# A two-block transformer kernel: x loaded and turned alone, weights split ahead of norms, and the second block's modulation summed between other products

## The reference

```
for i in range(DEPTH):
    mod_lat = (silu(c) @ w_mod[i] + b_mod[i])      # 6144 values: sh1, sc1, gt1, sh2, sc2, gt2
    mod_ctx = (silu(c_ctx) @ w_mod[i] + b_mod[i])
    hc = modulate(rms_norm_2(x_ctx, g_norm1[i]), csh1, csc1)   # modulate: h * (1 + scale) + shift
    h  = modulate(rms_norm_2(x_lat, g_norm1[i]), sh1, sc1)
    ... input projection, attention over both streams, pooling, mix ...
    x_lat = x_lat + gt1 * mix
    x_lat = x_lat + gt2 * sq_relu_mlp(modulate(rms_norm_2(x_lat, g_norm2[i]), sh2, sc2), w_mlp1[i], w_mlp2[i])
    if not last: the same for x_ctx
```

## Time and profile before

| | |
|---|---|
| median of 3 runs | 2930.61 us |
| the runs | 2924.84 to 2932.65 us |
| the profiled execution, its own time | 2934.35 us |
| its span, first to last instruction | 2932.6 us |
| mean granted clock | 0.954 |
| TensorE, VectorE, ScalarE, POOL busy | 94%, 52%, 30%, 3% of the span |
| data moved | 415.47 MB, 142 GB/s on the mean |

### The profile page before, as it was taken

How to read it: one execution, slowest core, us unless ns; L and a number is a source line. 1 busy time by engine, 2 the same in 40 slices (tenths; PEclk the granted TensorE clock), 3 DMA queues, 4 the chain that set the end, 5 groups by cost and what they waited for, 6 DMA issues and landing times. The chain is left out here.

```text
span 2932.6 us, 42259 instructions
## 1 busy us (share of the span) xinstructions
PE 2746.5 (94%) x17731; PEld 2370.5 (81%) x17731; DVE 1517.5 (52%) x2131; ACT 878.1 (30%) x1141; POOL 99.1 (3%) x179
## 2 busy tenths in 40 slices
PE   6999988999989999889999979899899999879998
PEld 6998887889989998778889934355799997636898
DVE  5774553427867844543257721452555553244555
ACT  3332201123333322101223321442333332243332
POOL 1100000000100000000001000000000000000000
PEclk8999989999999999989999989889999999989999
DMA  6775201635766764005347552000355455210452
GB/s 224 264 257 173 87 1 44 201 112 181 268 213 231 264 206 138 1 1 187 114 155 254 201 203 86 29 1 29 101 175 194 148 184 198 78 43 15 144 173 86
DMA packets 279067, 415.47 MB, mean 142 GB/s; under 512 B 10057, under 2 KB 235545, under 8 KB 277266
## 3 DMA queue, kind: packets, MB, share of 16 engines
q1 hardware_dynamic: 259948, 348.17, 36.1%
q0 software_dynamic: 18128, 64.20, 6.4%
q10 hardware_dynamic: 854, 1.13, 0.1%
HBM read 399.82 MB, written 13.65 MB: 141 GB/s over the span
## 5 line engine op out<-in xcount | busy, mean ns | idle before, releaser
L533 PE MATMUL ps<-h_high,w_high 128*128 128x256 f32 x1408 | 403.2, 286 | 17.1 <-DVE h_low L1169 10.3
L534 PE MATMUL ps<-h_low,w_high 128*128 128x256 f32 x1408 | 402.6, 286 | 0.0
L535 PE MATMUL ps<-h_high,w_low 128*128 128x256 f32 x1408 | 402.4, 286 | 0.0
L1190 DVE TENSOR_TENSOR w_low<-ring,w_high 128x2048 fp32r<-128x2048 f32 x132 | 302.1, 2290 | 136.1 <-ACT w_high L986 135.7
L629 PE MATMUL ps<-h_sb,ring 128*128 128x256 f32 x1472 | 328.0, 384 | 15.9 <-issue 9.3
L2404 DVE TENSOR_TENSOR w_low<-ring,w_high 128x2048 fp32r<-128x2048 f32 x96 | 219.8, 2291 | 222.9 <-ACT w_high L2231 222.9
L986 ACT ACTIVATE w_high<-ring 128x2048 fp32r<-128x2048 f32 x132 | 251.7, 1914 | 267.0 <-DMA ring<-in_ffn_w_in 152.6
L629 PEld LDWEIGHTS ps<-h_sb,ring 128*128 128x128 f32 x1472 | 282.9, 193 | 59.1 <-issue 17.3
L533 PEld LDWEIGHTS ps<-h_high,w_high 128*128 128x128 f32 x1408 | 274.8, 195 | 18.6 <-issue 11.4
L2231 ACT ACTIVATE w_high<-ring 128x2048 fp32r<-128x2048 f32 x96 | 183.9, 1915 | 313.6 <-PE ps L1935 313.6
L534 PEld LDWEIGHTS ps<-h_low,w_high 128*128 128x128 f32 x1408 | 274.8, 195 | 0.0
(11 more groups left out here) (380 smaller groups left out, 4654.8 us busy)
## 6 DMA issues: line engine op xcount, KB each, us to landing
ring<-in_w_mlp SPq DMA_DIRECT2D x96, 1024.0 KB, 5.3
ring<-in_ffn_w_in SPq DMA_DIRECT2D x88, 1024.0 KB, 8.5
wmod<-in_w_mod POOLq DMA_DIRECT2D x96, 512.0 KB, 6.5
ring<-in_ffn_w_out SPq DMA_DIRECT2D x44, 1024.0 KB, 5.0
ring<-in_w_mix_in SPq DMA_DIRECT2D x26, 1024.0 KB, 5.6
ring<-in_xattn_w_kv SPq DMA_DIRECT2D x16, 1024.0 KB, 5.4
mod_scratch<-mod_acc POOLq DMA_DIRECT2D x24, 512.0 KB, 5.5
ring<-mod_scratch SPq DMA_DIRECT2D x12, 1024.0 KB, 7.8
```

Source lines behind the costliest of these rows:

```text
L533: mm(dst, w_hi, x_hi, start=start, stop=False, **more)
L534: mm(dst, w_hi, x_lo, start=False, stop=False, **more)
L535: return mm(dst, w_lo, x_hi, start=False, stop=stop, **more)
L1190: v.tensor_tensor(w_low[:, slot, :], ring[:, slot, :], w_high[buffer], ALU.subtract).then_inc(w_low_ready.sem, 1)
```

## The change

In the front there is no block and no barrier any more. x is turned first, the squares follow on ScalarE (into `kt`, since `h_sb` holds the tokens), and the parameter rows are turned behind the sums of squares. Both tiles of the first feed-forward step are split ahead of the root (`first_high`, `first_low`); `cond` is made behind mem's norm. SP issues six weight tiles in place of three, POOL its loads, at once.

At the end of the first block SP loads the modulation's six tiles for layer 0 into the first block's ring (`MOD_SLOTS`, by when the slots come free). The second block sums two of them before the last norm's sums, one behind it, two behind the transposes, and the last behind the sums of both streams' first norm. Layer 1's tiles go through the second ring: two are summed ahead of the context's MLP of layer 0, four between the two MLPs (`MOD_BESIDE`), with the context's norm of layer 1 behind them. `mods` and `scls` are kept per layer.

In the output stage the sums of squares stand between the output tiles, the first two weight tiles are split ahead of the residual, and `scale` and `low` alternate per k. The MLP's first up tile goes k by k over both halves, its last down tile bank by bank (`acc_done`), and a start flag takes the place of the cleared banks. The output leaves in four quarters, of which ScalarE copies one.

```diff
 MEM_BANKS = (5, 6, 7, 0)
+MOD_SLOTS = (3, 4, 5, 0, 1, 2)
...
+MOD_BESIDE = ((0, 1), (2, 3, 4, 5))
...
     def _(pe):
+        pe.wait_ge(const_loaded.sem, 16)
+        pe.wait_ge(loaded.sem, 16)
+        for q in range(4):
+            for k in (2 * q, 2 * q + 1):
+                for h in range(2):
+                    at = (k % 2) * T + h * P
+                    last = nc.tensor.transpose(ps[q][:, at:at + P], x_tok[:, h, k * P:(k + 1) * P], ident)
+            last.then_inc(*x_turned.up())
         tensor_program(pe)
...
             if n == 0 and l == 0:
-                w_high_part(FfnTiles(0, 0), 0, 0, 0, 0)
+                act.wait_ge(*rows_turned.at(0, 1))
+                first_high(0, 0)
             act.wait_ge(*ss_done.at(l, n + 1))
...
+        sp.wait_ge(mod_stored.sem, MOD_CHUNKS * 16)
+        for s in MOD_SLOTS:
+            sp.wait_ge(w_used[s].sem, DEPTH * FIRST_USES[s] + 1)
+            c, t = divmod(s, MOD_THIRDS)
+            sp.dma_start(ring[:, s, :], scratch["mod"][0, :, c, t * SLOT:(t + 1) * SLOT]
+                         ).then_inc(store["v_loaded"][s].sem, 16)
...
+        def mod_sums(i, n, first, final):
+            r, used = loaded(("mod", i, n))
+            if i == 0:
+                r = store["ring"][:, n, :]
+            for m in range(SLOT // PIECE):
+                row = n * (SLOT // PIECE) + m
+                last = mm(ps[7][0:MOD_ROWS, :], one_row[:, MOD_ROWS - 1 - row:2 * MOD_ROWS - 1 - row],
+                          r[:, m * PIECE:(m + 1) * PIECE], start=(first and m == 0),
+                          stop=(final and m == SLOT // PIECE - 1))
+            last.then_inc(used.sem, 1)
...
-            norm(i, 1, streams(i))
-            for c in streams(i):
-                mlp(i, c)
-            layer_ends(i)
+                if j:
+                    for s in streams(i):
+                        sums(i, 1, s, j - 1)
+            for s in streams(i):
+                sums(i, 1, s, 3)
+            if i < DEPTH - 1:
+                for n in MOD_BESIDE[CTX]:
+                    mod_sums(i + 1, n, n == 0, False)
+            mlp(i, streams(i)[0])
+            if i < DEPTH - 1:
+                for n in MOD_BESIDE[LAT]:
+                    mod_sums(i + 1, n, False, n == MOD_BESIDE[LAT][-1])
+                for q in range(4):
+                    sums(i + 1, 0, CTX, q)
+                mod_turn(i + 1)
+                mlp(i, LAT)
+                for q in range(1, 4):
+                    sums(i + 1, 0, LAT, q)
...
+            mlp(i, streams(i)[0])
+            if i < DEPTH - 1:
+                w_low_part(MlpTiles(i, LAT), 0, 0, 0, 0)
+                residual(CTX)
+                w_low_part(MlpTiles(i, LAT), 0, 1, 1, 1)
                 dve.wait_ge(*x_ready.now(0))
-            layer_ends(i)
+                modulate(i + 1)
+                for k in range(KD):
+                    scale(i + 1, 0, CTX, k)
+                mlp(i, LAT)
+            residual(LAT)
```

More of the change, by code:

```diff
@@ L288, in build_first @@
     ring = sb("ring", [P, RING, SLOT])
+    store["ring"] = ring
     h_sb = sb("h_sb", [P, KD, T])
@@ L957, in norm @@
         def norm(l, n):
-            squares = cat if n == 3 else h_sb
+            squares = squares_of(l, n)
             if n == 3 or (n == 0 and l):
@@ L1580, in build_first @@
+    half = [name for name, _ in PARAMS[:9]]
     block = ctx.enter_context(nc.Block())
@@ L1583, in _ @@
     def _(sp):
+        sp.dma_start(x_tok, w_dram["x"].rearrange("o (h p) n -> p (o h) n", p=P)).then_inc(loaded.sem, 16)
+        sp.dma_start(cst["all"], w_dram["consts"]).then_inc(const_loaded.sem, 16)
+        load_rows(sp, [name for name, _ in PARAMS if name not in half])
         sync_program(sp)
@@ L1768, in build_second @@
     turned, placed = sig("second_turned"), sig("second_placed")
-    w_loaded = [sig(f"v_loaded{s}") for s in range(RING2)]
+    w_loaded = store["v_loaded"]
     w_used = [sig(f"v_used{s}") for s in range(RING2)]
@@ new lines, in square, with root @@
+        def square(i, n, s):
+            for q in range(4):
+                act.wait_ge(*x_ready.at(*x_needed(i, n, s, q)))
+                go(squares[s][:, 2 * q:2 * q + 2, :], xs[s][:, 2 * q:2 * q + 2, :], ACT.Square
+                   ).then_inc(*sq_ready.up())
+        def root(i, n, s):
+            act.wait_ge(*ss_done.at(i, norm_at(i, n, s) + 1))
+            go(std[:, s, :], norm_sum(i, n, s), ACT.Ln, bias=eps[:, 0:1], scale=1.0 / D).then_inc(*std_ready.up())
+            act.wait_ge(*std_ready.now(0))
+            go(std[:, s, :], std[:, s, :], ACT.Exp, scale=-0.5).then_inc(*std_ready.up())
@@ new lines, in shift, with first_high @@
+        def shift(i, n, s, k):
+            act.wait_ge(*scaled.at(i, scaled_at(i, n, s, k)))
+            dst = h_high[s][:, k, :] if n else h[:, k, cols(s)]
+            go(dst, h[:, k, cols(s)], ACT.Identity, bias=mods[i][:, s, n * 3 * KD + k:n * 3 * KD + k + 1]
+               ).then_inc(*h_ready.up())
+        def first_high(tiles):
+            if tiles.index:
+                s, use = place(("mlp2", tiles.i, CTX, MLP_STEPS - 2))
+                w_high_part(tiles, 0, 0, 0, 0, (w_used[s].sem, use + 1))
+                s, use = place(("mlp2", tiles.i, CTX, MLP_STEPS - 1))
+                w_high_part(tiles, 0, 1, 0, 1, (w_used[s].sem, use + 1))
+            else:
+                w_high_part(tiles, 0, 0, 0, 0)
+                w_high_part(tiles, 0, 1, 0, 1)
@@ L2240, in tile @@
                     before = tiles.used(*before)
-                elif tiles.index:
-                    s, use = place(("mlp2", i, streams(i)[tiles.index - 1], MLP_STEPS - 1))
-                    before = (w_used[s].sem, use + 1)
                 w_high_part(tiles, r, q, j, parity, before)
@@ L2273, in scalar_program @@
             ub, ask = unit_base(i), asked(i)
-            norm(i, 0, (CTX, LAT))
+            if i == 0:
+                for s in (CTX, LAT):
+                    square(i, 0, s)
+                for s in (CTX, LAT):
+                    root(i, 0, s)
+                for k in range(KD):
+                    for s in (CTX, LAT):
+                        shift(i, 0, s, k)
+            else:
+                square(i, 0, LAT)
+                root(i, 0, LAT)
+                for k in range(KD):
+                    shift(i, 0, LAT, k)
             for n, (j, _, width) in enumerate(IN_TILES):
@@ L2410, in tile @@
             def tile(r, q, j, t, parity, before):
-                if not (tiles.index == 0 and isinstance(t, int) and t == 1):
+                if not (isinstance(t, int) and t == 1):
                     w_low_part(tiles, r, q, t, parity)
```

460 lines of the change are left out of this document (234 added, 226 removed).

## The result

After takes 2843.95 us (median of 4, 2842.53 to 2863.51) against 2931.58 before (2924.84 to 2932.65): ratio 0.9724, interval 0.9695 to 0.9754. I had forecast 2871 and a range of 2862 to 2884.

The account below looks back on a forecast made before the run. TensorE, busy 94% of the span, was taken as the bound; 4.6 + 15.9 + 33.3 + 2.1 + 3.7 = 59.6 us off 2934.35 gave 2874.8, or 2871 us beside the median 2930.6. Range: 2862 to 2884.

Parts of the forecast that it names:

- Front: Start up to the first feed-forward matmul: earlier transposes and sums bring it from 34.1 to 29.5 us, saving 4.6 us.
- My upper bound, 6: Largest saving given for the start of the kernel: 6 us, if the clock rises within the sums.
- Between the blocks: First block's last matmul to first input projection: modulation matmuls cover waits, lost time falls from 20.8 to 4.9, saving 15.9 us.
- Layer 0 to layer 1: Block two, layer 0's MLPs to layer 1's projection: 36.2 us lost, new idle 2.9, saving 33.3 us.
- Layer 1's MLP 2.1 and the end 3.7: Shorter `h_low` wait at the last MLP saves 2.1 us; output by banks and quarters, with ScalarE's copy, saves 3.7 us.
- Its whole worth is TensorE time that was idle or slow at seven seams: Basis of the sum: no weight matmul removed or added; only seam time counts, less new waits, 59.6 us in all.
- signs that I had named for the profile after: First `h_high` matmul at 28 to 31 us, shorter seams, no idle between layer 0's MLPs, block two's waits under 5 us.
- rival C: The shorter pauses left (1.7 to 2.9 us) leave the clock up, saving more behind the projections: 2865 us; chance 0.12.
- Rival A: The sum of seam savings holds as it stands, 2871 us within some 5 us; chance 0.60.
- B's holes: Covers taken for full have holes, such as a late split tile; two of 3 us cost 10 us: 2881; chance 0.22.
- D's late tiles: Modulation tiles wait in SP's queue behind MLP weights and cover nothing: 2925 us, no change; chance 0.03.
- E's tiring clock: A fuller TensorE is granted less clock, in the MLPs from 2080 us on: slower, up to 2946 us; chance 0.03.

Follow-up runs that it names:

- e11: After, with two extra ScalarE squares of x ahead of its first squares, so that TensorE pauses between transposes and sums: 2859.41 us.
- e7: After, with ScalarE's three loads in layer 1 of the first block again issued ahead of the squares of the first norm: 2857.27 us.
- e3: Before, with filler matmuls of constants in the two pauses ahead of block two's score and value matmuls, four per layer: 2911.64 us, ratio 0.9938.
- e12: After, with filler matmuls of constants that fit the attention-stage pauses of block two, and more at three of its seams: 2826.93 us, ratio to before 0.9650.
- e10: After, with extra ScalarE squares to put a pause back ahead of both input projections of block two (missed its place in layer 0): 2860.05 us.
- e15: After, with three half-width filler matmuls (1.28 us) behind the first input projection tile of layer 0: 2868.30 us.
- e6: After, with two filler matmuls of 0.86 us each behind the first input projection tile, in both layers: 2856.98 us.
- e17: After, with the tile by tile wait undone: TensorE waits for all of h ahead of the first input tile, both layers: 2876.55 us.
- e16: Before, with only the tile by tile wait for the latents' shifted h in the first input tile added: 2921.35 us, ratio 0.9969.
- e1: The kernel before, unchanged, traced a second time: 2931.18 us.
- e5: Before, with two filler matmuls of 0.86 us each behind the first input projection tile, in both layers: 2932.84 us.
- e13: Before, with one half-width filler matmul (0.43 us) behind the first input projection tile of layer 0 alone: 2931.55 us.
- e14: Before, with two half-width filler matmuls (0.86 us) behind the first input projection tile of layer 0: 2929.74 us.
- e4: After, with too many filler matmuls in all five larger pauses of each attention stage of block two, running over the pauses: 2848.24 us.

## Why the prediction was wrong

The sum had the right sign and the right seams, and it was short by 30 us in the profiled executions (27 in the medians): 26 of the 30 in stages for which it had no term.

- **Front, 4.6 forecast, 8.5 measured.** The step that failed is "the sums, whose squares ride behind the copies, 6.4 at the low clock". That 6.4 was the price behind a pause of 4.84 us; after has none there, and they took 3.62. e11 put the pause back and got 5.94. My upper bound, 6, named this case but priced it at half. The other 1.2 us: they began at 12.2, not 12.8, and the chain behind them was 0.6 shorter.
- **Between the blocks, 15.9; measured 15.3.** Right, pause by pause (1.66, 0.87, 2.45 for 1.7, 0.9, 2.3).
- **Layer 0 to layer 1, 33.3; measured 33.7.** Right. The MLPs and the modulation run without a gap, no split tile and no residual came late:

```profile
2039.47:2241.00 201.53, 201.53 (x1584) 1.00 0.56 193
2241.00:2425.00 184.00, 184.00 (x1533) 1.00 0.52 174
```

- **Layer 1's MLP 2.1 and the end 3.7; measured 2.2 and 4.0.** Right.
- **The sum as a whole, and the larger failure.** The step is "Its whole worth is TensorE time that was idle or slow at seven seams": it took for granted that what the change does not touch keeps its length and its clock. It did not: the value stages gave 14.9 and 6.3 us, the projection and norms of layer 0 took 1.9 back (mean granted clock 0.90, before 0.91), and layer 1 of the first block gave some 3 to 4 through an edit that I left out (ScalarE's three loads behind the squares; of that the pause, 1.6 us, is shown in e7, the rest is read off two of its executions). The first block scatters by itself: 1647.6 to 1654.0 us in eight traces of before and its variants (mean 1651.3), 1645.2 to 1650.6 in ten of after's (mean 1647.0, e7 left out), so of the 5.7 in the two traces about 4 belong to the change.

Of the signs that I had named for the profile after, all came but one: the first `h_high` matmul stood at 25.6, not at 28 to 31.

What stands behind the 21 us, and how firmly. Shown: the low stretch is entered at the two pauses ahead of the stage (e3, and e12 beside e10), and the same code falls into it or not with 0.6 us of difference in where the clock stands on arrival (e7, one trace, beside four of after's seam). Delays of 1.3 and 1.7 us at the first input tile bring it back too (e15, e6). Shown too: in this change the tile by tile start of the projection is needed for value stages at 2.4 GHz (e17) and does not bring them about alone (e16). So the 21 us came by the moment of arrival, at which no step of the change aimed: as a design they are luck, and four fillers per layer gave before the same two lengths (e3). Argued only: how before corrects a delay. Several of its low stretches begin inside a pause of fixed length; if a start comes later, the pause ends later and less work falls into the stretch, so about half of the delay is given back, at each such stretch. That fits 0.38 of 0.43, 0.80 of 0.98 and all of 1.7 us. It would make the arrival of each kernel a fixed point, and before's lies on the side of the fall. This fits it too: in six traces with before's code up to there (before, e1, e3, e5, e13, e14) the low stretch about the first projection begins 2.8 to 3.1 us ahead of it, in eight with after's (all but e7) 1.4 to 1.6, although the first block's length differs by 6 and by 5 us among them. Open: which other edits move after's point to the other side, and why e6 fell with its last rise at 4.04 us, 0.02 from a trace that did not.

The Trainium skill, TensorE: Matmul & The Clock Gate (Why this matters for your kernels), asks that pauses be kept short. Here the clock stayed up through a pause of 1.66 us, and it fell at pauses of 2.45 and 2.23 us, which are shorter than those that the page warns of; the measurement decides. Windows from the end of the first of these pauses to the fall, and behind it:

```profile
1675.69:1711.70 36.01, 34.31 (x118) 1.00 0.65 230
1711.90:1718.50 6.60, 5.17 (x6) 0.50 0.94 298
```

So rival C, too, was wrong in its premise, although its time, 2865, lay nearer. Rival A's mechanism was right at the seams and missed the rest; B's holes, D's late tiles and E's tiring clock did not show.

## What to carry to other kernels

Cut the trace into stages and look at each for its granted clock, also at those that a change leaves alone: a stage of small matmuls behind a pause may run at either clock for tens of microseconds, and a shift of under 2 us elsewhere can switch it. Where that is so, guard the entry with fillers that fit the pause. It gave 18 us to before; in after, whose value stages were fast already, fillers in the pauses of norms and seams gave 17. Fillers longer than the pauses took their gain back (e4). And don't carry a duration over to a place with another pause ahead of it.

## What the hardware showed that I had not expected

- TensorE stayed at 1.2 GHz for 33.75 us while 33.62 of them were busy, on matmuls of 64 to 128 rows and 128 to 256 columns, and ran the same work at 2.4 GHz when it came in fast. The Trainium skill, TensorE: Matmul & The Clock Gate (What's actually happening), has the fast clock return soon once the array is busy; here it did not, and the measurement decides. (39.50 us in e15.)
- Two executions of one kernel agree to 0.05 us per stage over 1200 us, low stretches included, although they reach the seam 1.4 to 2.5 us apart.
- In before a delay of 0.43 to 1.7 us of TensorE's own work was gone within the next 160 us, but for 0.02 to 0.18 us (e5, e13, e14).
- The same code after the same seam took 97.0 or 116.7 us in its value stage, with 0.6 us between the moments of arrival (after, e7).
